# Recurrent channels regrouped so that each gate head is one 96x96 product

## The reference

```python
z = jnp.einsum("bsd,de->bse", rms_norm(x, g_mix), w_in) + b_in
va, ga, xb, gb, sa, sb = jnp.split(z, cuts, axis=-1)     # xb and gb: 1536 channels each
v = causal_depthwise_conv(xb, conv_b_w, conv_b_b)        # 4 taps
xh = v.reshape(bsz, s, 16, 96)                           # 16 heads of 96 channels
r = sigmoid(einsum("bshi,hij->bshj", xh, w_rg_a) + b_rg_a)
i = sigmoid(einsum("bshi,hij->bshj", xh, w_rg_x) + b_rg_x)
log_a = -8 * r * softplus(-lam)
a = exp(log_a); bterm = sqrt(1 - a*a) * i * v            # the factor is 1 at the first token
h[t] = a[t] * h[t-1] + bterm[t]
y_b = einsum("bsc,cd->bsd", h * gelu(gb), w_b_out)
```

## Time and profile before

| | |
|---|---|
| time of three runs | 2678.05 us median (2676.75 to 2680.03) |
| profiled execution | 2678.74 us, of which 2677.0 us are the span of the trace |
| granted clock of PE, mean | 0.973 |
| busy: PE, PEld | 2530.9 us (95%), 2046.1 us (76%) |
| busy: DVE, ACT | 1386.7 us (52%), 811.0 us (30%) |
| gate matmuls (L598) | 97.4 us busy |
| DMA | 133 MB, 50 GB/s, 17% of the time of the 16 engines |

### The profile page before, as it was taken

The page is one execution under the profiler, slowest core; times in us unless marked ns, Lnnn a source line. Parts: engine busy times, 40 slices in busy tenths (PEclk is TensorE's granted clock), DMA queues, the critical chain, the costliest instruction groups (busy, mean ns, idle before and its releaser), DMA issues.

```text
span 2677.0 us, 26736 instructions
## 1 busy us (share of the span) xinstructions
PE 2530.9 (95%) x11412; PEld 2046.1 (76%) x11412; DVE 1386.7 (52%) x1671; ACT 811.0 (30%) x1204; POOL 2.8 (0%) x7
## 2 busy tenths in 40 slices
PE   7999999999999479999999999999989999999778
PEld 5686868688888248788888888888878777878567
DVE  5574665598899974233233232332565334541366
ACT  4434352512122152333122131231332232221354
POOL 0000000000000000000000000000000000000000
PEclk9999999999999779999999999999899999999889
DMA  3111102011111002211111111121112111111401
GB/s 124 34 51 31 56 20 64 18 54 55 48 48 48 16 16 60 79 44 55 48 48 52 45 54 47 48 63 47 49 36 64 40 32 40 48 47 48 134 10 70
DMA packets 228025, 133.18 MB, mean 50 GB/s; under 512 B 12730, under 2 KB 224954, under 8 KB 227906
## 3 DMA queue, kind: packets, MB, share of 16 engines
q1 hardware_dynamic: 227906, 131.47, 16.9%
HBM read 125.12 MB, written 6.32 MB: 49 GB/s over the span
## 4 chain that ended last, share of the span: by engine, by line
PE 81%; DVE 12%; ACT 4%; issue 1%; SPq 1%; DMA 1%; ACTq 0%; DVEq 0%
PE bank L531 24%; PE bank L533 24%; PE bank L532 24%; DVE uc L1529 4%; PE bank L598 4%; DVE sa L1529 2%; PE bank L565 1%; DVE wlo L1398 1%; DVE u_in L1529 1%; PE bank L681 1%; PE bank L762 1%; PE bank L778 1%; PE bank L668 1%; DVE tmp L1752 0%; DVE uc L1645 0%
## 5 line engine op out<-in xcount | busy, mean ns | idle before, releaser
L531 PE MATMUL bank<-h_hi,whi 128*128 128x512 f32 x2000 | 786.8, 393 | 0.3 <-DVE h_lo L1413 0.3
L533 PE MATMUL bank<-h_hi,wlo 128*128 128x512 f32 x2000 | 779.8, 390 | 0.0
L532 PE MATMUL bank<-h_lo,whi 128*128 128x512 f32 x2000 | 779.7, 390 | 0.0
L531 PEld LDWEIGHTS bank<-h_hi,whi 128*128 128x128 f32 x2000 | 376.5, 188 | 81.1 <-issue 2.2
L532 PEld LDWEIGHTS bank<-h_lo,whi 128*128 128x128 f32 x2000 | 376.5, 188 | 80.9 <-issue 3.1
L533 PEld LDWEIGHTS bank<-h_hi,wlo 128*128 128x128 f32 x2000 | 376.3, 188 | 78.8
L895 ACT ACTIVATE whi<-raw 128x1024 fp32r<-128x1024 f32 (+2 forms) x212 | 216.6, 1023 | 460.8 <-PE bank L533 456.9
L1398 DVE TENSOR_TENSOR wlo<-raw,whi 128x1024 fp32r<-128x1024 f32 (+2 forms) x212 | 251.2, 1185 | 180.4 <-ACT whi L895 179.5
L1529 DVE SCALAR_TENSOR_TENSOR uc<-u_in,par,uc 128x1024 f32<-128x1024 f32 x163 | 205.3, 1280 | 1.1
L531 PE MATMUL bank<-ff_hi,whi 128*128 128x512 f32 x512 | 199.9, 390 | 0.0
L533 PE MATMUL bank<-ff_hi,wlo 128*128 128x512 f32 x512 | 199.3, 389 | 0.0
(11 more groups left out here) (335 smaller groups left out, 3164.1 us busy)
## 6 DMA issues: line engine op xcount, KB each, us to landing
raw<-in_w_in SPq DMA_DIRECT2D x92, 512.0 KB, 3.8
raw<-in_w SPq DMA_DIRECT2D x64, 512.0 KB, 3.9
raw<-in_w_b_out SPq DMA_DIRECT2D x16, 384.0 KB, 3.1
raw<-in_w_out SPq DMA_DIRECT2D x11, 512.0 KB, 3.4
x_in<-in_x SPq DMA_DIRECT2D x8, 512.0 KB, 5.3
raw<-in_w_a_out SPq DMA_DIRECT2D x8, 512.0 KB, 3.9
raw<-in_w_o SPq DMA_DIRECT2D x8, 512.0 KB, 3.7
xcols<-in_x SPq DMA_DIRECT2D x16, 256.0 KB, 2.7
```

The lines of the kernel that those rows point to most:

```text
L531: pe.matmul(target, lh, rh, start=start, stop=False, skip_group_check=True)
L532: pe.matmul(target, lh, rl, start=False, stop=False, skip_group_check=True)
L533: last = pe.matmul(target, ll, rh, start=False, stop=stop and point is not None, skip_group_check=True)
```

## The change

The channels of a group are laid out anew. Tile t of a group (t = 0, 1, 2) now holds head t on partitions 0 to 95 and the t-th third (32 channels) of the group's fourth head on partitions 96 to 127. Gate heads 0 to 2 are one 96x96 product each on partitions 0 to 95 of their tile. For head 3 its three thirds are first copied by ACT into one 96-partition tile `fourth`; its two gates are computed from there (`gate_tile(g, GT)` on PE) into `fourth_gate`, and ACT copies a third of each back to partitions 96 to 127 of T1 and T3 of every tile. A group then has 16 gate matmuls in the place of 28. The columns of w_in, the rows of w_b_out and the parameters of the recurrent channels are loaded in the new order, which takes two DMAs (96 and 32 wide) where one was. The gate weights are two DMAs in a group, for 20 before, and the two POOL memsets that cleared them are gone. The rest of the diff renames or moves rows of tables.

The loads (SP and the tables they go by):

```diff
         def need_rnn(kind, col, g, t):
-            need((kind, g, t), w_in, 0, DT, col + (g * GT + t) * P, P)
+            number[kind, g, t] = len(blocks)
+            first, rest = col + g * GROUP_RNN + t * HEAD, col + g * GROUP_RNN + GT * HEAD + t * PART
+            rows_ = lambda c, n: w_in[:, c:c + n].rearrange("(k p) c -> p k c", p=P)
+            blocks.append(([(slice(0, P), (0, HEAD), rows_(first, HEAD)), (slice(0, P), (HEAD, P), rows_(rest, PART))], DT, P))
...
+        for name, column in [("b_in", Z_XB), ("b_in", Z_GB), *RNN_ROWS.items()]:
...
+            for t in range(GT):
+                for c0, c1, source in ((0, HEAD, t * HEAD), (HEAD, P, GT * HEAD + t * PART)):
...
+                        row_pieces[at_row // P].append((rows_in[at_row // P][first:first + GT * (m - 1) + 1:GT, c0:c1],
+                                                        groups[done:done + m, source:source + c1 - c0]))
...
             def load_gates(g):
-                for n in range(2):
-                    w.wait_ge(*at("gate_w_clear", n))
...
+                for n, name in enumerate(("w_rg_a", "w_rg_x")):
+                    w.wait_ge(*(at("gate", g - 1, 3, n, 1) if g else at("x", DT - 1, 1)))
+                    sp.dma_start(gate_w[n][:], A[name][0, 4 * g:4 * g + 4].rearrange("q r c -> r q c")).then_inc(
```

The matmuls on PE:

```diff
             def gate_tile(g, c):
-                rows_ = [a for a, cc in PAIRS if cc == c]
+                source, point = (v[c][0:HEAD, :], ("rnn_in", g, c)) if c < GT else (fourth[:], ("fourth", g, GT - 1))
                 for n in range(2):
                     w.wait_ge(*at("gate_w", g, n))
                     for half in range(2):
                         b = bank("gate", g, c, n, half)
...
+                        w.wait_ge(*at(*point))
+                        pe.matmul(b[0:HEAD, :], gate_w[n][:, c, :], source[:, cut(half)], start=True, stop=True).then_inc(
...
                 for t in range(1, GT):
                     block(("gb", g, t), h, "h")
+                gate_tile(g, GT)
                 gate_tile(g, 0)
```

ACT:

```diff
+            def fourth_in(g, t):
...
+                act.activation(fourth[t * PART:(t + 1) * PART, :], v[t][HEAD:P, :], ACT.Copy).then_inc(*did(("fourth", g, t)))
+
+            def fourth_gates(g):
+                for n in range(2):
+                    for half in range(2):
...
+                        act.activation(fourth_gate[n][:, cut(half)], bank("gate", g, GT, n, half)[0:HEAD, :], ACT.Tanh,
...
             def gate_tile(g, c):
...
+                w.wait_ge(*at("fourth_gate", g, 0, 1))
+                act.activation(T1[HEAD:P, :], fourth_gate[0][part, :], ACT.Copy).then_inc(*did(("fourth_moved", 0, j)))
...
+                w.wait_ge(*at("fourth_gate", g, 1, 1))
+                act.activation(T3[HEAD:P, :], fourth_gate[1][part, :], ACT.Copy).then_inc(*did(("fourth_moved", 1, j)))
...
                 for t in range(1, GT):
                     gb_tile(g, t)
+                for t in range(GT):
+                    fourth_in(g, t)
+                fourth_gates(g)
                 gate_tile(g, 0)
```

More of the change, by code:

```diff
@@ L286, in build_program @@
         T1, T2, T3 = (sb(f"lru{i}", "g", o + 4096 * i, [P, SEQ]) for i in range(3)); o += 3 * 4096
[L287 to L297, removed]
+        gate_w = [sb(f"gate_w{n}", "g", o + 1536 * n, [HEAD, 4, HEAD]) for n in range(2)]; o += 2 * 1536
+        fourth = sb("fourth", "g", o, [HEAD, SEQ]); o += 4096
+        fourth_gate = [sb(f"fourth_gate{n}", "g", o + 4096 * n, [HEAD, SEQ]) for n in range(2)]; o += 2 * 4096
+        fourth_bias = small[:, 180:188]
         EDGE = [0, 4224 + 16 * 4096]
@@ L413, in ahead @@
                         w.wait_ge(*at("cleared"))
-                    for n, ((c0, c1), src) in enumerate(pieces):
+                    for n, (ps, (c0, c1), src) in enumerate(pieces):
                         point = [("raw", i)] if n == len(pieces) - 1 else []
-                        sp.dma_start(view[:, :, c0:c1], src).then_inc(*landed(f"raw{i % 2}", *point))
+                        sp.dma_start(view[ps, :, c0:c1], src).then_inc(*landed(f"raw{i % 2}", *point))
             def load_rows(s):
@@ L444, in sync @@
                 load_rows(s)
+            for n, name in enumerate(("b_rg_a", "b_rg_x")):
+                for g in range(NG):
+                    first = g * GROUP_RNN + GT * HEAD
+                    sp.dma_start(fourth_bias[0:HEAD, 4 * n + g:4 * n + g + 1], A[name][:, first:first + HEAD].rearrange("l c -> c l")
+                                 ).then_inc(*landed("fourth_bias", ("fourth_raw", n, g)))
             sp.dma_start(mask[:], A["mask"]).then_inc(*landed("mask", ("mask",)))
@@ L595, in gate_tile @@
                         b = bank("gate", g, c, n, half)
-                        for m, a in enumerate(rows_):
-                            w.wait_ge(*at("rnn_in", g, a))
-                            last = pe.matmul(b[:], gate_w[n][:, PAIRS.index((a, c)), :], v[a][:, cut(half)], start=m == 0,
-                                             stop=m == len(rows_) - 1)
-                        last.then_inc(*up("pe_done", ("gate", g, c, n, half)))
+                        w.wait_ge(*at(*point))
+                        pe.matmul(b[0:HEAD, :], gate_w[n][:, c, :], source[:, cut(half)], start=True, stop=True).then_inc(
+                            *up("pe_done", ("gate", g, c, n, half)))
             for t in range(GT):
@@ L998, in conv_input @@
                     if j < 2:
-                        w.wait_ge(*at("gate", NG - 1, 1 if j == 0 else 2, 1, 1))
+                        w.wait_ge(*at("gate", NG - 1, j, 1, 1))
+                        w.wait_ge(*at("fourth", NG - 1, j))
                         w.wait_ge(*at("v_scaled", (NG - 1) * GT + j))
@@ L1459, in xb_tile @@
                 if g:
-                    w.wait_ge(*at("gate", g - 1, 1 if t == 0 else 2, 1, 1))
+                    w.wait_ge(*at("gate", g - 1, t, 1, 1))
+                    w.wait_ge(*at("fourth", g - 1, t))
                 for m in range(TAPS_B):
@@ L2062, in gpsimd @@
             w = Once(pool)
-            w.wait_ge(*at("x", DT - 1, 1))
-            for n in range(2):
-                pool.memset(gate_w[n][:], 0.0).then_inc(*up("pool_done", ("gate_w_clear", n)))
             w.wait_ge(*at("w", number["gates"] - 2))
```

87 lines of the change are left out of this document (58 added, 29 removed).

## The result

The changed kernel takes 2757.57 us (median of four runs, 2754.42 to 2761.74), the kernel before, run beside it, 2678.54 us. The ratio is 1.0298 (95% interval 1.0285 to 1.0311): 79 us or 3.0% slower. The forecast had the sign and the mechanism, but its 2736 us and its range up to 2752 lie too low. The profiled execution has a span of 2757.9 us against 2677.0, so 80.9 us are to be found. It is one of the longer executions of the changed kernel.

A forecast was written before the change was run, and what follows sets the result against it. PE was taken to bound the recurrent groups, with little slack against the ACT/DVE chain, and DVE the taps behind. Start 9.8 + three groups 33.3 + last group and taps 14.6 = +57.7 us, so 2736 us, range 2704 to 2752.

The forecast's parts named there:

- PE's three stops in a group: Groups 0 to 2: PE idle 9.0 us before fourth's first product, 2.2 before xb 0, 6.8 inside gate tile 2.
- DVE's taps as the bound behind: Behind the last group: DVE's late taps delay va 2's low weights, so va 2 starts 13.1 us late; then taps bind.
- late loads: Rival for weight loads: at six times today's landing, blocks xb and gb stop PE, 2776 us; 0.05 together with dearer clock.
- The start: +9.8 us: Start of the kernel: 28 more parameter-row DMAs on SPq ahead of x's last six tiles; bounds 8 and 11 us.
- for the small ones I take 0.35: Start: issue price of 0.35 us for each small parameter-row DMA; bounds 0.29 and 0.4.
- The clock of PE ... another 3.2 / 2 = 1.6 us: PE: a stop over about 3 us lowers the clock and costs another 1.6 us of work; bounds 0 and 3.
- +11.1 us: Each of groups 0 to 2: standing 9.0 + 2.2 + 6.8, clock 3.1, less 10.0 for twelve products; three groups +33.3 us.
- The copies: ACT in each gate stage: 0.95 us per 32x1024 copy, three into fourth, two back per tile; bounds 0.25 and 1.06.
- +14.6 us: Group 3 and the taps: va 2 starts 13.1 us late, plus 1.6 for the clock, given as +14.6 us.
- the products are what counts: Rival for the groups: the chain would not stop PE, only 39.8 us of saved products count, 2649 us; chance 0.04.
- the clock does not fall: Rival for PE's stops: no or less clock loss, 2724 us, or 2703 with copies of 0.25 us; chance 0.19.
- The dearer clock: Case for PE's stops: 3 us of clock instead of 1.6 at about nine stops, 12.6 us more; 0.05 with late loads.

The follow-up runs named there:

- x5_again: Repeat of x5_contig (changed kernel, narrow parameter pieces written to neighbouring partitions instead of every third): 2746.34 us, ratio 1.0256 to the kernel before.
- c1_fill: Changed kernel plus ten gate products with overwritten sums on PE ahead of the first product on fourth in each group: 2747.26 us, ratio 1.0258.
- x6_nomove: Changed kernel without ACT's two copies back to partitions 96 to 127 in each gate tile: 2736.13 us, ratio 1.0216.
- c2_fill2: Changed kernel plus five useless gate products on PE during the wait inside gate tile 2, groups 0 to 2: 2751.11 us, ratio 1.0272.
- b1_diag: Kernel before with only the diagonal piece of each gate tile, 12 gate products a group instead of 28: 2677.15 us, ratio 0.9995.
- v1_direct: Changed kernel with fourth's products added straight into each tile's bank, no copies back, early input copies, most parameter rows behind x: 2684.86 us, ratio 1.0024.
- x3_start: Changed kernel with most parameter rows loaded behind x and their transposes moved behind block xb 1 of group 0: 2735.15 us, ratio 1.0212.
- x5_contig: Changed kernel with narrow parameter pieces written to neighbouring partitions instead of every third: 2747.44 us (median of three executions), ratio 1.0262.

## Why the forecast was right in kind and too low

Right: PE's three stops in a group, their places and their releasers; the clock lowered behind them; the groups (not the loads) as the place of most of the cost; DVE's taps as the bound behind, with va 2 late; narrow loads of weights without cost. None of PE's stops in the groups or behind them is released by a load or its split, except by two late low parts behind the last group (0.41 and 2.84 us), which DVE makes between its taps; the loads of 384 and 128 KB land in 3.3 and 3.5 us; and the packets of queue q1 take 16.9% of the engines' time, as before. The rule of the Trainium skill (DMA: Bandwidth & Descriptors, "Specifications") on transfers under 512 bytes thus didn't decide here. The time lies above 2752, to which the forecast gave 0.05, and not for late loads: two terms were too small.

- **"The start: +9.8 us" failed.** It measured 18.9. The step that failed is "for the small ones I take 0.35", with bounds 0.29 and 0.4: it took the price of a piece on neighbouring partitions, as the rows of before had no other. A piece on every third partition costs 0.62 (the changed kernel against x5_again). That is 9.1 us of the 24.1 by which the stages together exceed the forecast's 57.7.
- **"The clock of PE ... another 3.2 / 2 = 1.6 us" failed in size, and so "+11.1 us".** Group 1 stood 9.26 + 2.33 + 5.72 = 17.3 us, where the forecast has 18.0; twelve products fewer are 12 x 0.86 = 10.3, for 10.0. That leaves 136.8 - 123.0 - 17.3 + 10.3 = 6.8 us, where 3.1 were counted. Rows show 5.6 of them as clock: 2.6 for the first stop (c1_fill), 1.6 for the second (x6_nomove) and 1.4 for the third (c2_fill2), for 1.6, 0 and 1.5; the other 1.2 no row explains. The forecast counted a stop only above about 3 us, and a stop of 2.33 costs 1.6. And it took the recovery of the one long idle time of before, 3.2 us, for every stop; behind the first stop it took 5.0 to 6.1 us, behind the third 3.8 to 7.0. Over groups 0 to 2 the clock costs 8.1 + 4.8 + 5.7 = 18.6 us for 9.3, and the three groups are 43.2 for 33.3: 9.9 us more.
- **The copies were nearly right.** 1.08 us each in a row for 0.95, two of them 2.4 in the chain for 1.9, since each waits for the end of the one ahead. The exp came 1.9 us later than forecast: 1.2 by the clock during the products on fourth, 0.26 by the copies in, 0.5 between the end of these products and the exp, where the copies back lie. x6_nomove confirms nearly all of their price. The budget of the Trainium skill (ScalarE: Activation LUTs, "Rules for kernel authors"), 1.15 us by estimate, lies 0.07 above the 1.08 measured, and my 0.95 lay 0.13 below it; the Trainium skill states that budget for a bias given as a pointer operand, and the copies have none.
- **"+14.6 us" for the last group measured 19.7.** va 2 begins 139.8 us after the group's start, before 123.0: 16.8 late for 13.1. That is the chain's own delay: the 1.9 us above, 0.8 more in this group's products on fourth, and 0.5 for the copies of each of two tiles. Behind its stop of 2.84 us the clock is low for 6.0 us, which costs 3.0 for the forecast 1.6.
- **The rival "the products are what counts"** had 0.04 and fell twice, in b1_diag and v1_direct. The rival "the clock does not fall" fell with c1_fill and c2_fill2. The dearer clock was in the range's upper bound, with 3 us a stop, but the start's bound of 11 us was too low, and both went wrong in the same direction.

## What to carry to other kernels

Before products are saved, look for the chain of the other engines that runs beside them, and write down its slack: here it was 3.9 and 0.6 us, so work had to be moved into the gap first and could be removed only then. What is put ahead of a chain's first link (copies, tanh of an extra tile) costs most of its length at every pass, and a stop of the matmul engine can cost more than it lasts. Here those of 2.8 to 9.3 us cost 1.4 to 3.4 us on top, those of 2.3 to 2.6 us nothing or about as much; useless matmuls in the wait got that back in two places. Price a DMA issue by its pattern, not its bytes: take the row of a piece with the same stride, and if there is none, bound it from above by twice the nearest.

## What the runs showed of the hardware

- A DMA of 4 rows of 384 or 128 bytes to every third partition of SBUF holds SP's queue for 0.62 us, to neighbouring partitions for 0.34.
- PE's clock around an idle time, in the changed kernel: in group 1 full for 4.3 us of the stop of 9.26 (windows: 254 to 259 at 1.00, 259 to 262 at 0.51), and at 1.2 GHz until 5.3 us after the restart. After the stops of 2.33 us it was back 3.3 to 4.3 us after the restart, after those of 5.7 us 4.1, 3.8 and 7.0. A stop of 2.33 us lowered it in every group and not behind the last one (x3_start); in group 0 it fell only 0.5 us after PE had started again.
- Matmuls that compute nothing wanted kept the clock at 1.00 through a wait (c1_fill), and the kernel took 10 us less.
- One of the four executions of x5_contig took 11.1 ms: its trace has PE busy for 10998 us and DVE for 1402, about as ever. The two of x5_again show nothing of it, the cause is not known, and nothing here rests on it.
